# First layer's last tiles turned into other PSUM banks, MLP quarters staged by group, first projection unit reordered

## The reference, cut to what matters

```python
mix = jnp.concatenate([y_a, y_b, y_c, y_d], axis=-1) @ w_out[l]
h = layer_norm(DEEPNORM_ALPHA * h + mix, ln1_g[l], ln1_b[l])
ff = jnp.square(jax.nn.relu(h @ w_mlp1[l])) @ w_mlp2[l]     # 1024 -> 4096 -> 1024
h = layer_norm(DEEPNORM_ALPHA * h + ff, ln2_g[l], ln2_b[l])
```

## Time and profile before

| | us |
|---|---|
| median of the runs before | 2842.62 (2842.02 to 2843.44, 3 runs) |
| the profiled execution | 2847.2 |
| its span in the profile | 2845.4 |
| TensorE busy in it | 2720.9 (96%) |
| VectorE busy | 1790.9 (63%) |
| ScalarE busy | 1136.3 (40%) |

### The profile page before, as it was taken

The page is one execution under the profiler, slowest core; times in us unless marked ns, Lnnn a source line. Parts: engine busy times, 40 slices in busy tenths (PEclk is TensorE's granted clock), DMA queues, the critical chain, the costliest instruction groups (busy, mean ns, idle before and its releaser), DMA issues. The chain is left out here.

```text
span 2845.4 us, 37143 instructions
## 1 busy us (share of the span) xinstructions
PE 2720.9 (96%) x13986; PEld 2183.4 (77%) x13986; DVE 1790.9 (63%) x2939; ACT 1136.3 (40%) x1817; POOL 252.0 (9%) x220
## 2 busy tenths in 40 slices
PE   5999989999989999999999999899999899999997
PEld 5899866656868887888888998566568688878886
DVE  5654554454787776776856444535547877758778
ACT  3322223334355554433433222234343555543343
POOL 3121222000000000000011112220000000000000
PEclk9999989999999999999999999799999999999998
DMA  4223234102315445997621233421032354479875
GB/s 164 71 68 94 91 92 92 31 1 82 103 64 176 143 144 192 384 312 247 225 86 38 77 100 97 101 54 30 1 119 89 97 163 145 141 261 364 290 230 188
DMA packets 254360, 387.29 MB, mean 136 GB/s; under 512 B 38608, under 2 KB 126800, under 8 KB 254184
## 3 DMA queue, kind: packets, MB, share of 16 engines
q1 hardware_dynamic: 254184, 384.92, 42.3%
HBM read 288.05 MB, written 96.83 MB: 135 GB/s over the span
## 5 line engine op out<-in xcount | busy, mean ns | idle before, releaser
L2747 ACT ACTIVATE att_PT<-att_ST 128x512 f32<-128x512 f32 (+2 forms) x244 | 135.3, 554 | 327.3 <-PE att_ST L2639 196.0
L1626 PE MATMUL mix_acc<-mix_whi,x_hi 128*128 128x256 f32 (+1 forms) x640 | 185.5, 290 | 0.0
L998 PE MATMUL dense_tr<-mlp_w,mlp_a 128*128 128x512 f32 x448 | 175.9, 393 | 6.3 <-DVE mlp_w L1302 6.3
L1628 PE MATMUL mix_acc<-mix_whi,x_lo 128*128 128x256 f32 (+1 forms) x640 | 180.1, 281 | 0.0
L1627 PE MATMUL mix_acc<-mix_wlo,x_hi 128*128 128x256 f32 (+1 forms) x640 | 180.0, 281 | 0.0
L1000 PE MATMUL dense_tr<-mlp_w,mlp_a 128*128 128x512 f32 x448 | 174.9, 390 | 0.0
L999 PE MATMUL dense_tr<-mlp_w,mlp_a 128*128 128x512 f32 x448 | 174.9, 390 | 0.0
L998 PE MATMUL dense_acc<-mlp_w,mlp_a 128*128 128x512 f32 x448 | 174.4, 389 | 0.0
L999 PE MATMUL dense_acc<-mlp_w,mlp_a 128*128 128x512 f32 x448 | 174.4, 389 | 0.0
L1000 PE MATMUL dense_acc<-mlp_w,mlp_a 128*128 128x512 f32 x448 | 174.4, 389 | 0.0
L644 POOL TENSOR_TENSOR norm_rstd<-norm_var,norm_power 128x1 f32<-128x1 f32 x32 | 29.8, 932 | 1474.1 <-DVE norm_var L624 1474.1
(11 more groups left out here) (432 smaller groups left out, 7461.1 us busy)
## 6 DMA issues: line engine op xcount, KB each, us to landing
mlp_w_raw<-w_mlp SPq DMA_DIRECT2D x124, 512.0 KB, 6.1
blocks<-h SPq DMA_DIRECT2D x32, 1792.0 KB, 8.4
mlp_a_raw<-blocks SPq DMA_DIRECT2D x72, 512.0 KB, 4.5
mlp_raw<-w_mlp SPq DMA_DIRECT2D x66, 512.0 KB, 6.1
ahead<-w_in SPq DMA_DIRECT2D x20, 1024.0 KB, 6.6
mlp_temp<-blocks SPq DMA_DIRECT2D x38, 512.0 KB, 4.9
residual<-h SPq DMA_DIRECT2D x32, 512.0 KB, 3.9
h<-residual SPq DMA_DIRECT2D x32, 512.0 KB, 9.7
```

The costliest lines, as they stand in the source:

```text
L998: pe.matmul(out, ah, wh, start=(ch == 0 and k == 0), stop=False, skip_group_check=True)
L1626: pe.matmul(out, xh, whi[b][:, k, 0:n], start=(k == 0), stop=False)
L1628: mm = pe.matmul(out, xl, whi[b][:, k, 0:n], start=False, stop=(k == KT - 1))
L2747: act.activation(PT[0:width, n % 3, c0:512], ST[0:width, n % 2, c0:512], ACT.Exp).then_inc(s.exp_ready, 1)
```

## The change

Three parts.

1. `turn_h` and the splits of the first layer: for tiles 4 to 7 the first half of the tile goes to `banks[0][t - 4]`, the bank out of which the tile's own last sum was just added, with no wait beyond that for the norm. The second half goes to `tr[:, 1, :]` and `acc[:, 1, :]` by turns and waits for the low halves of the tile two before.
2. The quarters (0, 1) and (1, 0) of group g lie in slots 6 and 5 of `stage[g % 2]`. `activate` waits for the store of group g - 2 where it waited for `block_sums(g - 1)`. `block_sums` goes in the order 2, 5, 1, 6, 7, with waits on itself before the two that overwrite a quarter. The work of group 1 moves up from step 14 to step 13, on ACT and DVE, and `block_sums(0)` moves from step 13 to step 14. It holds for both layers.
3. Unit 0 of `mixers` (both layers) does a pair of k steps with the high weights when `first_hi` is there, and the matmuls with the low weights one pair later, after `first_lo`.

```diff
-        a12, a21 = flat[:, 14 * 512:15 * 512], flat[:, 15 * 512:16 * 512]
+        a12_of, a21_of = (lambda g: stage[g % 2][:, 6, :]), (lambda g: stage[g % 2][:, 5, :])
...
-        norm_banks = (tr[:, 1, :], acc[:, 1, :])
+        norm_bank = lambda t, half: (tr[:, 1, :], acc[:, 1, :])[half if t < HT else t % 2] if t < HT or half else banks[0][t - HT]
...
                     for half in range(2):
                         g = 2 * (m - NT) + half
-                        if g >= 2:
-                            pe.wait_ge(s.h_lo, g - 1)
+                        if t < HT:
+                            if g >= 2:
+                                pe.wait_ge(s.h_lo, g - 1)
+                        elif half:
+                            pe.wait_ge(s.h_lo, 2 * HT if t < HT + 2 else 2 * t - 2)
...
                 def activate(g, i):
-                    if g:
-                        act.wait_ge(s.blocks_ready, g)
+                    if g >= 2:
+                        act.wait_ge(blocks_stored[g % 2], 16 * (g // 2))
                     else:
+                        act.wait_ge(s.z_turned, NT)
...
                         elif i == 2:
                             if g == 2:
-                                activate(1, 4)
-                                activate(1, 3)
                                 square(1, 6)
                             square(g - 1, 7)
...
                     elif (g, i) == (1, 7):
                         square(0, 7)
+                        activate(1, 4)
+                        activate(1, 3)
...
-                    for i in (1, 2, 5, 6, 7):
+                    for n, i in enumerate((2, 5, 1, 6, 7)):
                         (a, b), op = PRODUCTS[i].left
+                        if i in (6, 7):
+                            dve.wait_ge(s.quarter_read, 2 * g + n - 2)
                         mm = dve.tensor_tensor(stage[g % 2][:, i - 1, :], part[a], part[b], op)
+                        if i in (2, 5):
+                            mm.then_inc(s.quarter_read, 1)
...
                         elif (g, i) == (2, 2):
-                            rests(1)
-                            quarter22(1)
-                            quarter11(1)
-                    elif (g, i) == (0, 1):
-                        rests(0)
-                    elif (g, i) == (1, 7):
-                        block_sums(0)
+                            block_sums(0)
+                    elif (g, i) in ((0, 1), (1, 7)):
+                        gather(g)
+                        rest12(g)
+                        rest21(g)
+                        rest1(g)
+                        if g:
+                            quarter22(g)
                     if i == 6 and g != 1:
                         quarter22(g)
-                    elif i == 7 and g != 1:
+                    elif i == 7:
                         quarter11(g)
...
+                    if unit == 0:
+                        for part in range(5):
+                            if part < 4:
+                                pe.wait_ge(s.first_hi, part + 1)
+                                for k in (2 * part, 2 * part + 1):
+                                    pe.matmul(out, whi[b][:, k, cols], hi[:, k, half * 512:(half + 1) * 512], start=(k == 0), stop=False)
+                                    pe.matmul(out, whi[b][:, k, cols], lo[:, k, half * 512:(half + 1) * 512], start=False, stop=False)
+                            if part:
+                                pe.wait_ge(s.first_lo, part)
+                                for k in (2 * part - 2, 2 * part - 1):
+                                    mm = pe.matmul(out, wlo[b][:, k, cols], hi[:, k, half * 512:(half + 1) * 512], start=False, stop=(k == KT - 1))
+                        mm.then_inc(s.unit_done, 1)
+                        return
```

More of the change, by code:

```diff
@@ L877, in high_half @@
             act.wait_ge(s.h_turned, g + 1)
-            act.activation(hi[:, 4 * half:4 * half + 4, here(t)], by_rows(norm_banks[half]), ACT.Copy).then_inc(s.h_hi, 1)
+            act.activation(hi[:, 4 * half:4 * half + 4, here(t)], by_rows(norm_bank(t, half)), ACT.Copy).then_inc(s.h_hi, 1)
         def low_half(dve, m, half):
@@ L882, in low_half @@
             dve.wait_ge(s.h_hi, g + 1)
-            dve.tensor_tensor(lo[:, part, here(t)], by_rows(norm_banks[half]), hi[:, part, here(t)].bitcast(F32), MINUS).then_inc(s.h_lo, 1)
+            dve.tensor_tensor(lo[:, part, here(t)], by_rows(norm_bank(t, half)), hi[:, part, here(t)].bitcast(F32), MINUS).then_inc(s.h_lo, 1)
         with nc.Block() as block:
@@ L1009, in turn_h @@
                         g = 2 * (m - NT) + half
-                        if g >= 2:
-                            pe.wait_ge(s.h_lo, g - 1)
+                        if t < HT:
[3 more added lines that the diff above has]
+                            pe.wait_ge(s.h_lo, 2 * HT if t < HT + 2 else 2 * t - 2)
                         for j in range(4):
                             k = 4 * half + j
-                            mm = pe.transpose(norm_banks[half][:, j * P:(j + 1) * P], h[:, t, k * P:(k + 1) * P], ident[:])
+                            mm = pe.transpose(norm_bank(t, half)[:, j * P:(j + 1) * P], h[:, t, k * P:(k + 1) * P], ident[:])
                         mm.then_inc(s.h_turned, 1)
@@ L1074, in activate @@
                 def activate(g, i):
-                    dst, bank, relu, ready = (a12, tr[:, g % 2, :], s.relu12, s.ready12) if i == 4 else (a21, acc[:, g % 2, :], s.relu21, s.ready21)
+                    dst, bank, relu, ready = (a12_of(g), tr[:, g % 2, :], s.relu12, s.ready12) if i == 4 else (a21_of(g), acc[:, g % 2, :], s.relu21, s.ready21)
                     act.wait_ge(s.multiplied, at[g, i] + 1)
-                    if g:
-                        act.wait_ge(s.blocks_ready, g)
+                    if g >= 2:
+                        act.wait_ge(blocks_stored[g % 2], 16 * (g // 2))
                     else:
+                        act.wait_ge(s.z_turned, NT)
                         act.wait_ge(s.sum_ready, sum_at[7, HT - 1] + 1)
@@ L1231, in block_sums @@
                 def block_sums(g):
-                    part = {(0, 0): stage[g % 2][:, 2, :], (1, 1): stage[g % 2][:, 3, :], (0, 1): a12, (1, 0): a21}
+                    part = {(0, 0): stage[g % 2][:, 2, :], (1, 1): stage[g % 2][:, 3, :], (0, 1): a12_of(g), (1, 0): a21_of(g)}
                     dve.wait_ge(s.ready22, 2 * g + 2)
@@ L1653, in features_unit @@
                     out = bank_of(unit)[:]
+                    if unit == 0:
[11 more added lines that the diff above has]
+                        return
                     for k in range(KT):
-                        if unit == 0 and k % 2 == 0:
-                            pe.wait_ge(s.first_lo, k // 2 + 1)
                         xh, xl = hi[:, k, half * 512:(half + 1) * 512], lo[:, k, half * 512:(half + 1) * 512]
```

## The result

The changed kernel takes 2849.4 us (2848.14 to 2853.0, 8 runs) against 2842.31 us (2840.18 to 2843.82, 8 runs) for the kernel before. The ratio is 1.0028, with a 95% interval of 1.0019 to 1.0037. That is 5 to 11 us slower. I had said 2852.0, within 2845 to 2857.

The account below looks back on a forecast made before the run. TensorE is busy 96%, but the MLP's stall ends twice, the second end hanging on group 3's load. Terms +9.8 (part 2), +1.7 (clock), -0.7, -1.4 gave +9.4: 2852.0 us against the median of 2842.6, range 2845 to 2857.

Parts of the forecast that it names:

- What is late next: MLP, both layers: later `block_sums(0)` delays group 0's store and group 3's load; product 20 4.90 us late, +9.8 in all.
- The new wait of `activate`: MLP, ACT: the wait for group 0's store ends at about 861, before ACT comes at 864.7; costs nothing.
- Rival 2: MLP: group 3's load lands before DVE needs it, product 20 6.1 us earlier, whole kernel 2828.3; chance 0.05.
- The clock: TensorE after the gap before product 20: one drop to slow clock in one layer, +1.7 us; bounds 0 to 5.
- Part 1: End of the first layer: tile 6 starts when its norm ends, 0.66 us earlier; taken as -0.7, bounds 0 to -2.4.
- Part 3: Unit 0 of the mixers, both layers: TensorE starts 0.70 us earlier at the first high half, -1.4 in all.
- The load's price: Group 3's load: 2.8 MB in two DMAs lands 10.5 us after issue by the row, against the skill's 8.6.

Follow-up runs that it names:

- e9: Kernel before, with one added wait in SP's queue so group 0's store and group 3's load behind it leave later: 2858.77 us, ratio 1.0056.
- e5: Changed kernel with `block_sums(0)` put back in step 13, ahead of `gather(1)`: ratio 0.9978 to the kernel before.
- e3: Changed kernel with group 3's raw weights load issued before group 0's store in SP's queue: 2836.28 us, ratio 0.9975 to the kernel before.
- e7: e3 with group 2's two quarters in the eighth tile of `h`, so no store is waited for: 2827.1 us, ratio 0.9945 to the kernel before.
- e1: Kernel before with parts 1 and 3 of the change alone, the MLP untouched: 2836.68 us, ratio 0.9982.
- e6: Changed kernel with group 3's load issued ahead of group 0's store, but only after `block_sums(0)`: 2846.73 us, ratio 1.0013 to the kernel before.
- e2: Kernel before with part 2 of the change alone (quarters by group, moved steps): 2854.07 us, ratio 1.0039.

## Why the prediction was right

**What is late next (right).** The chain that the prediction followed came true step by step. Against the starts of product 12: the copy L1068 at 15.90 (847.29, against 19.88 before), 3.98 earlier (3.97 said); `block_sums(0)` 5.53 later (5.55); product 20 4.77 and 4.82 later than before (4.90); DVE's wait 10.92 (some 11); TensorE's 7.69 and 7.79 before product 19 (8). The experiments show that it is a cause and not only a chain: lateness alone does it (`e9`), and its removal undoes it (`e5`, `e3`, `e7`).

**The new wait of `activate` (right here, too short elsewhere).** That it costs nothing in the changed kernel holds, as ACT comes to it after the store has landed. In my expectation for the early load I then forgot it, although the prediction itself had put the landing of the store at 861. ACT stands before `activate(2, 4)` from 849.87 on in `e3`, which is 853.75 in the times of the kernel before, some 7 us ahead of that. `e3` showed it; `e7` took it away and gave the full amount. Rival 2, with its 2828 for an early load, has its condition wrong in the same way: the early load alone isn't enough.

**The clock (right in size, by luck in number).** I took one slow stretch, in one of the two layers, after the gap before product 20. It came in the second layer. The windows (columns as in the earlier trace rows) of product 19 up to the start of product 20, first and second layer, and of the start of the second layer's product 20:

```profile
861.40:868.00 6.60, 5.02 (x13) 3.72 (x13) 6.57 (x11) 4.10 (x9) 0.00 (x0) 0.68 0.43 146
2262.00:2268.50 6.50, 4.43 (x12) 3.26 (x12) 6.46 (x12) 4.00 (x9) 0.00 (x0) 0.76 0.41 141
2268.50:2271.90 3.40, 3.32 (x8) 2.68 (x9) 3.40 (x7) 1.09 (x2) 0.00 (x0) 0.50 1.04 279
```

From product 20 to 21 it is 2.83 us in the first layer and 4.39 in the second: 1.6 for the slow stretch, against 1.7 taken. That it was one and not none or two is luck, since nothing in my working told the gaps of the two layers apart (1.55 and 2.08 us). Over all twelve profiles the seven gaps before product 20 of up to 1.57 us were followed by no slow stretch, the seven of 2.08 us and more all were, and of three gaps of 1.77 to 1.79 one was. With this, part 2 cost 4.78 + 6.40 = 11.2 us in the profile, 11 by the runs of part 2 alone, 11.5 by my sum.

**Part 1 (the term that was too small).** I had -0.7, with -2.4 as the far bound. The turn of tile 6 now waits for the norm and starts 0.68 us earlier against the first projection (0.66 said); the wait before it is 2.45 us, a little longer than the old 2.39, so the gap only moved, as said. The step that failed is that I took the slow clock after this wait as given. TensorE's timeline (tile 5, tile 6, unit 0), and the window of the earlier trace rows again:

```profile
1440.12 1.09 PE L1019 MATMUL dense_acc<-ident,h 128*128 128x128 f32 x8 [0.86 <-DVE h L640]
1446.56 0.66 PE L1019 MATMUL dense_acc<-ident,h 128*128 128x128 f32 x4 [2.45 <-DVE h L640]
1465.20 0.51 PE L1665 MATMUL mix_acc<-x_hi,mix_whi 128*128 128x512 f32 x1 [2.29 <-ACT mix_whi L1904]
```
```profile
1448.30:1451.70 3.40, 3.40 (x31) 3.40 (x30) 3.02 (x5) 1.17 (x5) 0.00 (x0) 1.00 0.33 134
```

Where the kernel before ran at 0.50, this one runs at 1.00. From the first projection to the end of the last one the six kernels with the old turns take 32.50 to 32.74 us in their profiles, always with a slow stretch. Of the six with the new turns, three take 30.42 or 30.43, without one (the changed kernel, `e1`, `e7`), and three 31.94 to 32.00, with one (`e3`, `e5`, `e6`). So part 1 brings 0.7 when the slow stretch comes and 2.3 when it stays out, and it stayed out in half of the profiles. One to two us of the distance between my 9.4 and the measured 7.1 lie here; in the profiled execution the three parts add up to 11.2 - 2.3 - 1.4 = +7.5. Why the clock stays up is open: the shorter wait before tile 5 (0.86 for 1.56) stands in all six, also in the three where the clock fell, so it doesn't decide it alone, and no run tested it by itself.

**Part 3 (right).** Unit 0 starts 0.71 us earlier against the last projection (wait 2.29 for 3.02; in the first layer 2.03 for 2.76), where I had 0.70. In six of the seven profiles with the new unit 0 its first 3.4 us in the second layer ran at a mean granted clock of 0.56 to 0.72, in one (`e3`) at 1.00; with the old unit 0 it was 0.50 to 0.57.

**The load's price.** The landing after 10.4 us is that of the row of before (10.5). The 8.6 us that the Trainium skill's page "DMA: Bandwidth & Descriptors", section "Anatomy of one DMA — SWDGE (gpsimd) path", would give for 2.8 MB, an estimate by a formula for DMAs of another issuing engine, does not hold for this pair. For 1 MB the same formula gives an estimate of 4.4 us; with the load issued first and the store 0.4 us behind it (`e6`), the load took 6.4 and 7.4 us. So this is no price of a load that runs alone.

## What to carry to other kernels

When a stall is removed, write down the second chain that ends in the same place before counting the gain: here ACT's chain hid a load, and that load had next to no slack left (a landing 5.2 us later in `e9` put product 20 back by 5.2 us). A step that is moved takes with it what waits for it in a queue that nobody looks at: `block_sums(0)` went one step later on DVE, and a DMA issue list written by hand carried this to a load that has nothing to do with it. In such a list a load whose place is free early should stand ahead of a store whose data come late, and a buffer shared with a store needs a second look each time something in front of it gets faster.

## What the runs showed of the hardware that I had not expected

A wait of 2.45 us before the turn of tile 6 left TensorE's granted clock at 1.00 in three profiles and was followed by 3.4 us at 0.50 or 0.51 in three others (`e3`, `e5`, `e6`), with the same instructions around it. Likewise the wait before product 20 in the two layers of the `e2` kernel: 1.79 us with 4.42 from there to the next product in the first, 1.77 with 2.84 in the second. So the same gap may cost nothing or 1.6 us, and a sum over gaps of 1.5 to 2.5 us can't be surer than that.
